# ScalarE's root and sigmoids ahead of mark 3, and two expert slots moved across the border of a tile

## The reference, cut to what matters

```python
# RWKV-7 group: norm of kk, decay w and in-context rate a
w = -softplus(-(w0 + tanh(xw) @ w2)) - 0.5
a = sigmoid(a0 + xa @ a2)
g = sigmoid(xg) @ g2
kk = heads(k * k_k)
kk = kk / maximum(sqrt(sum(kk * kk, axis=-1, keepdims=True)), L2_EPS)
k = k * (1.0 + (a - 1.0) * k_a)
# then the recurrence over frames, the window attention, x = x + concat(...) @ w_out

# PEER block: 8 heads x 16 experts of 16384 for each frame
s1, s2 = q1 @ key1.T, q2 @ key2.T      # top 16 of each, top 16 of their sums -> expert, gate
u   = take(down, expert)               # rows of 1024
act = gelu(einsum('thed,td->the', u, t))
out = einsum('the,thed->td', gate * act, take(up, expert))
```

## Time and profile before

| | |
|---|---|
| time, median of 3 runs | 4018.62 us (4008.57 to 4030.76) |
| the profiled execution | 3980.27 us |
| its span, first to last instruction | 3978.5 us |
| PE, busy | 3053.6 us (77%) |
| DVE, busy | 2887.4 us (73%) |
| ACT, busy | 1419.0 us (36%) |
| POOL, busy | 1533.8 us (39%) |
| DMA, moved | 1424.83 MB, mean 358 GB/s |
| granted clock of PE, mean | 0.878 of full speed |

### The profile page before, as it was taken

The page is one execution under the profiler, slowest core; times in us unless marked ns, Lnnn a source line. Parts: engine busy times, 40 slices in busy tenths (PEclk is TensorE's granted clock), DMA queues, the critical chain, the costliest instruction groups (busy, mean ns, idle before and its releaser), DMA issues.

```text
span 3978.5 us, 43460 instructions
## 1 busy us (share of the span) xinstructions
PE 3053.6 (77%) x13880; PEld 1740.0 (44%) x13880; DVE 2887.4 (73%) x6010; ACT 1419.0 (36%) x4020; POOL 1533.8 (39%) x1323
## 2 busy tenths in 40 slices
PE   7999977778777877687778677867777778776556
PEld 4655645445453535263526353635353535352112
DVE  2221468688869886988698769976897788778775
ACT  2111133424433353335243524352435242523223
POOL 1333134333334433444244324432443244334554
PEclk9999989888898889898989898979987988888779
DMA  7234379998999999999989998999899989999998
GB/s 263 99 126 159 107 315 404 408 375 359 400 410 378 375 395 416 371 368 411 417 336 401 409 416 334 404 405 413 342 404 404 398 356 386 408 370 391 420 420 354
DMA packets 243305, 1424.83 MB, mean 358 GB/s; under 512 B 27763, under 2 KB 53107, under 8 KB 95606
## 3 DMA queue, kind: packets, MB, share of 16 engines
q0 software_dynamic: 170784, 1223.91, 76.1%
q1 hardware_dynamic: 61222, 180.44, 11.9%
q10 hardware_dynamic: 11072, 17.70, 1.3%
HBM read 1389.02 MB, written 34.17 MB: 358 GB/s over the span
## 4 chain that ended last, share of the span: by engine, by line
DVE 31%; PE 28%; DMA 13%; ACT 7%; issue 6%; POOL 1%; DVEq 0%; POOLq 0%; PEldq 0%; ACTq 0%
DVE ex_rows L1604 14%; PE mx_ps L1590 11%; DMA ex_rows<-experts,mx_expert 8%; PE mx_ps L1254 5%; DMA mx_xs<-w_q 3%; DVE mx_acc L1614 3%; DMA mx_ex<-w_out 2%; PE mx_ps L1032 2%; PE mx_ps L1039 1%; PE mx_ps L1237 1%; PE mx_ps L1035 1%; PE mx_ps L996 1%; POOL ex_rows L1549 1%; ACT ex_diag L1570 1%; DVE mx_pqb L1355 1%
## 5 line engine op out<-in xcount | busy, mean ns | idle before, releaser
L1549 POOL DMA_INDIRECT ex_rows<-experts,mx_expert x1152 | 1404.7, 1219 | 2064.3 <-PE mx_ps L1590 1241.7
L1590 PE MATMUL mx_ps<-ex_rows,ex_diag 128*128 128x512 f32 x2740 | 1481.1, 686 | 407.1 <-ACT ex_diag L1570 394.9
L1604 DVE CUSTOM_DVE_ANT_0 ex_rows<-ex_rows,mx_acc 128x1024 f32<-128x1024 f32 x1152 | 1374.2, 1222 | 209.6 <-DMA ex_rows<-experts,mx_expert 191.3
L1590 PEld LDWEIGHTS mx_ps<-ex_rows,ex_diag 128*128 128x128 f32 x2740 | 556.6, 216 | 1169.0 <-issue 1161.8
L1560 ACT ACTIVATE ex_coef<-ex_coef 128x1 f32<-128x1 f32 x1152 | 220.2, 201 | 1499.0 <-DVE ex_coef L1604 1496.5
L1614 DVE SCALAR_TENSOR_TENSOR mx_acc<-ex_rows,ex_coef,mx_acc 128x1024 f32<-128x1024 f32 x467 | 599.2, 1283 | 63.3 <-ACT ex_coef L1563 53.2
L1413 PE MATMUL mx_ps<-pj_w,pj_hT 128*128 128x432 f32 x768 | 294.0, 541 | 5.8 <-ACT mx_acc L1426 4.7
L1563 ACT ACTIVATE ex_coef<-ex_coef,mx_gate 128x1 f32<-128x1 f32 x1152 | 283.9, 284 | 10.6
L1570 ACT ACTIVATE ex_diag<-cn_ident,ex_coef 128x128 f32<-128x128 f32 x685 | 255.5, 393 | 10.7
L1413 PEld LDWEIGHTS mx_ps<-pj_w,pj_hT 128*128 128x128 f32 x768 | 147.3, 195 | 139.1 <-issue 136.4
L1560 ACT ACT_TABLE_LOAD x137 | 175.8, 1283 | 13.2 <-DVE ex_coef L1604 10.2
(11 more groups left out here) (316 smaller groups left out, 3847.6 us busy)
## 6 DMA issues: line engine op xcount, KB each, us to landing
mx_fac<-w_q SPq DMA_DIRECT2D x54, 512.0 KB, 11.9
mx_ex<-w_out SPq DMA_DIRECT2D x36, 512.0 KB, 10.3
mx_ex<-w_q SPq DMA_DIRECT2D x36, 512.0 KB, 12.0
ex_rows<-experts,mx_expert POOLq DMA_INDIRECT x1152, 11.1
mx_p_cur<-w_q SPq DMA_DIRECT2D x27, 512.0 KB, 14.0
mx_xs<-w_q SPq DMA_DIRECT2D x27, 512.0 KB, 15.5
proj_rows<-mx_acc ACTq DMA_DIRECT2D x48, 216.0 KB, 1.9
mx_fac<-w_out SPq DMA_DIRECT2D x18, 512.0 KB, 18.3
```

What stands on the lines that cost most here:

```text
L1549: pool.indirect_dma_start(rows[:, g % RING, :], None, A["experts"], bass.IndirectOffsetOnAxis(expert[:, t % 2, s:s + 1], 0))\
L1590: last = pe.matmul(bank(6 + c), diag[:, diags.due(t, n) % DIAGS, :], up[:, r, c * 512:(c + 1) * 512], start=n == 0, stop=n == len(on_pe(t) ...
L1604: dve.tensor_tensor_reduce(out=down[:, r, :], in0=down[:, r, :], in1=tn[:, :], scale=1.0, scalar=0.0, op0=ALU.mult, op1=ALU.add, accum_out ...
```

## The change

STAGES gives two slots fewer to marks 60 to 67 (where DVE works out the expert numbers), one more to MARKS + 2, which had none, and one more to END. ACT's mark 3 goes from ahead of the root to the place of marks 4 and 5, so that root and sigmoids come right behind the copies of loraT. The product for kk's gain becomes a function of its own; PE calls it ahead of the loop and at the end of each turn but the last, ahead of the last marks' additions, and within the mix only for the sample tile.

```diff
-          (67, 13, 0.0),
+          (67, 11, 0.0),
           (71, 4, 0.2),
-          (MARKS + 1, 1, 0.2), (MARKS + 2, 0, 0.2), (MARKS + 3, 5, 0.2), (END, 5, 0.2))
+          (MARKS + 1, 1, 0.2), (MARKS + 2, 1, 0.2), (MARKS + 3, 5, 0.2), (END, 6, 0.2))
...
                .then_inc(loraT_ready.sem, 1)
-            slots.upto(3)
             act.wait_ge(kk_ss.sem, kk_ss.due(t, 1))
             act.activation(small[:, 1, :], small[:, 0, :], ACT.Sqrt).then_inc(kk_norm.sem, 1)
...
+        def key_gain(pe):
+            pe.matmul(bank(4), ones(KK_ROW), g2b[KK_ROW:KK_ROW + 1, :], start=True, stop=True,
+                      tile_position=(KK_ROW, 0)).then_inc(kkc_out.sem, 1)
+
         def mix_tensor(pe, t, m, slots):
...
-            pe.matmul(bank(4), ones(KK_ROW), g2b[KK_ROW:KK_ROW + 1, :], start=True, stop=True,
-                      tile_position=(KK_ROW, 0)).then_inc(kkc_out.sem, 1)
+            if sample:
+                key_gain(pe)
...
                 pe.sem_inc(tile_end.sem, 1)
+                key_gain(pe)
                 ahead = None
                 for t in range(T):
...
                     pe.sem_inc(tile_end.sem, 1)
+                    if t + 1 < T:
+                        key_gain(pe)
                     slots.upto(MARKS)
```

## The result

| | before | after |
|---|---|---|
| median | 4022.52 us (4008.57 to 4031.3, 9 runs) | 4044.94 us (4030.15 to 4056.75, 9 runs) |
| the profiled execution | 3980.27 us | 4046.4 us |
| its span | 3978.5 us | 4044.6 us |
| PE, busy | 3053.6 us | 3137.5 us |
| granted clock of PE, mean | 0.878 | 0.866 |

The ratio of after to before is 1.0066 (95% interval 1.0044 to 1.0088). The change makes the kernel slower by some 22 to 27 us, where 3 us of gain were forecast.

The account below looks back on a forecast made before the run. No one thing bounds a turn; what counts is when VectorE and PE get through the border. Gains of 1.2 + 2.6 + 0.4 - 1.4 = 2.8 us took 4018.62 to 4015.8 us, range 3990 to 4036.

Parts of the forecast that it names:

- L797's wait: VectorE's idle for kk's root at the border, 3.88 us in each of turns 2 to 7, would go.
- Turn 1: Keeps its slots; VectorE's 2.93 us wait for the root goes, and 2.6 us are gained.
- turn 0's wait: VectorE's 2.55 us wait for the root, while rows are only arriving; 0.4 us of gain kept.
- The products from L979 on: PE's products from L976 on in the old numbers, 6.4 us before; taken as 5.6, between 3.9 and 6.4.
- the forecast's sign of the moved slot: On PE, L1590's group in front of L989 would have 40 records instead of 32.
- The wait that the change adds: Turns 2 to 7: slot 127's gather waits until PE adds slot 116; L803 starts 3.1 us later.
- the four before took 4.2 us: PE's lora products from L971 keep their earlier 4.2 us, so the sigmoids end 7.5 us earlier.
- rival 2: Lora products at the lower clock, 8.4 us instead of 4.2; six turns lose 39 us, 4056 us; chance 0.13.
- the late row: The row of slot 127, wanted by VectorE at 2465.0 and landing at 2472.1, behind PE's addition of slot 116.
- Rival 1: Slot 127 in time at the border: VectorE's whole idle goes, 26 us gained, 3992 us; chance 0.17.
- Rival 3: ScalarE, held at mark 2 by slot 116's dot, reaches the root no sooner; 4019 to 4030 us; chance 0.05.
- The wait of VectorE at the dot of 127: One idle of 7.1 us ahead of L803 takes the place of waits of 3.9, 0.2 and 3.3.

Follow-up runs that it names:

- both on PE: The changed kernel, but slots 115 and 116 are both added by PE; 4027.33 us, ratio 1.0026 to the kernel before.
- neither on PE: The changed kernel, but slot 116 is added by VectorE like slot 115; 3997.03 us, ratio 0.9935 to the kernel before.
- slots alone: The kernel before with the new table of slots and the old order of ScalarE and PE; 4084.62 us, ratio 1.0131.
- exchanged adders: The changed kernel, but VectorE adds slot 116 and PE adds slot 115; 3986.3 us, ratio 0.9921 to the kernel before.
- kk's gain alone: The kernel before with only the product for kk's gain moved to the end of the turn before; 4023.29 us, ratio 1.0017.
- second look at before: The kernel before, unchanged, profiled a second time; 4015.9 us, ratio 0.9997, span 4003.6 us.
- order alone: The changed order of ScalarE and early product for kk's gain, with the old table of slots; 3991.42 us, ratio 0.9935 to the kernel before.

## Why the prediction was wrong

**Right, by its own steps.** L797's wait is gone in turns 1 to 7. Turn 1 gains 2.7 us (forecast 2.6), turn 0's wait loses 0.5 (forecast 0.4). The stretch ahead of the shifts of turns 2 to 7 is shorter by 21.3 us (3.55 each: 1.23 up to L1361, 2.32 behind it; forecast 3.5). The products from L979 on take 5.5 to 6.3 us, 5.9 in the mean (forecast 5.6). Forty records follow L983 in two groups of 20 (the forecast's sign of the moved slot), the gather starts 2.78 us behind the first of them (forecast 2.8), the exponentials hide, and L1626 stands behind the factors. The wait that the change adds was named with its place, its releaser and what is queued behind it.

**The step that failed** is the term "the four before took 4.2 us" for the lora products (the paragraph on ScalarE). It took the pace of the earlier trace rows, where PE comes to L971 straight from slot 117. The paragraph on rival 2 says itself that no slot is left to fill that place. In turns 2 to 7 of after, PE idles 2.15 us there and the stage from L974 to the sigmoids takes 6.1 to 8.1 us: the sigmoids start 13.0 to 15.0 us after the shift, 14.2 in the mean, where 11.3 was forecast. These 3.0 us go straight into the late row, and six times 3.0 is 18 us: by the account, borders and stretches ahead of turns 2 to 7 lose 18.7 us where 1.2 of gain were forecast. The steps behind held in sum: L979 to L802 took 16.1 to 17.2 us, forecast 16.35 (at this turn the landing was 6.16 instead of 5.6). So L802 comes 30.7 to 32.4 us after the shift, forecast 28.7.

With 18 us more the forecast would have been 4034, at the upper end of its range of 4036. The rest, to 4045, is in part the base (the median of before is 4022.5 over nine runs, 4018.6 over the three that stood ahead); the last 7 us I can't place, and neither can the account. The us or so per turn by which even the case with products at full pace fell short (both on PE: 2 us lost in six turns and turn 1, forecast about 4 gained) is between L802 and the factors: with both slots on PE, VectorE has two additions there where the forecast has one, and L1626 starts 41.0 us after its shift, forecast 40.1.

**Rival 2** had the mechanism and was too dear: it took all four products at the lower clock (8.4 us, measured 7.4 in the mean up to the sigmoids), L976 on at 6.4 (measured 5.9 at this turn) and the first slot slow too (it isn't: 8.83 us for 20 records, 0.44 each). Between it (4056) and the forecast (4016) lies the result. Its evidence against, that L971 ran at the full clock in turns 0 and 1, was the wrong row: in those turns PE had no idle ahead of it.

The Trainium skill's page "TensorE: Matmul & The Clock Gate" (What's actually happening) says that the throttled clock is the default state and that activity releases it. The rows agree for the most part. Where PE had idled 0.43 us or less ahead of these products (turns 2 to 7 of seven profiles, 42 in all), no pair took over 1.65 us. Where it had idled 1.2 to 2.2 us (18 turns: the change, neither on PE, slots alone), a pair of 2.0 us or more came in 15. But the other three, all with the slots alone, stayed at the full clock; here is one of them below a turn of the same profile that fell:

```profile
1286.88 2.08 PE L971 MATMUL mx_ps<-cn_w2a,mx_loraT 128*128 128x512 f32 x2 [2.14 <-ACT mx_loraT L701]
...
1696.62 1.13 PE L971 MATMUL mx_ps<-cn_w2a,mx_loraT 128*128 128x512 f32 x2 [2.12 <-ACT mx_loraT L701]
```

Behind the same idle, the granted clock over the four pairs was 0.50 in the first and 1.00 in the second. The idle that the change opened goes with the lower clock, but doesn't settle it alone; what else does stays open.

**Rival 1** fell as a forecast, but its size was right: without the late row the kernels gain 0.65 to 0.8%, 26 to 32 us, where it said 26. **Rival 3** fell: the root starts at 2500.71, 8.1 us after the shift, where 8.3 was forecast.

**Wrong without weight.** The wait of VectorE at the dot of 127 was forecast as one of 7.1 us; in five of turns 2 to 7 it is 10.1 in the mean, longer by the 3 us above. At the turn of 2492 us it is 5.45, because the four dots ahead of it wait for their own rows, 4.1 us in all: these rows land one in 2.49 us (dots at 2509.98 and, two rows on, 2514.95). The pace of the rows stays a limit when the late row is gone: with exchanged adders L802 comes 22.6 to 26.8 us after the shift, and not at the 21.6 at which VectorE alone would be (28.7 less the 7.1). At the end of the kernel, from the last L1361 on, 2.5 us more were forecast, and the profile shows 1.3 less (367.3 and 366.0 us).

## What to carry to other kernels

Where gathers are issued in order into a ring, count the slots from a blocking step to the end of the tile: if they are one more than the ring holds, the last gather, and all behind it in the queue, waits for an addition on the far side of that step. Ask which engine frees that row and what stands in its queue ahead of it; handing the row to the other engine (one number of the table) changed 0.66% of loss into 0.8% of gain. And a duration taken from a row holds only with what the engine did just before it (and, as the slots alone show, not always then): if the change takes that work away, take the row of the other case, or price the step at both clocks.

## What the runs showed of the hardware

The same products can take 1.7 times as long in one turn as in another of the same run, with nothing of the kernel changed. In the run with kk's gain alone, the stretch of two turns from L1047 to L1103 in the numbers of before, small state products for the most part, with the same 256 records of PE (columns: length, busy PE, PE's granted clock, DMA share, GB/s):

```profile
2177.80:2214.70 36.90, 36.40 (x256) 0.51 0.73 278
2583.10:2604.70 21.60, 20.87 (x256) 0.92 0.94 366
```

PE is busy all the time in both; in the first it ran the whole stretch at 0.51 of full speed, and its activity didn't bring the clock back. Which turns fall differs from run to run, and the sums over turns 2 to 7 from L1047 to L1119 lay between 306 and 389 us in ten profiles without following the ratios (343.9 in the second look at before, 357.4 after the change, 360.3 with the order alone, which is faster; the 389 belong to the slots alone, the slowest). Of the 66 us by which the profiles of before and after differ, where the medians differ by 22, 51 are from this stretch. What decides it stays open.

A gather of 1 MB behind a pause took 5.4 to 5.7 us from its issue to its dot in 17 of 18 cases (slot 127 in turns 2 to 7 of the change, of the slots alone and of both on PE), and 6.16 in the one shown above. The Trainium skill's page "DMA: Bandwidth & Descriptors" (Anatomy of one DMA — SWDGE (gpsimd) path) would give 4.4, an estimate from its fit; the measurement decides.
